# A state-space input made by channels and loaded in place, with the R transposes moved ahead of a g product

## The reference, cut to what matters

```python
z = jnp.einsum('bld,de->ble', h, w_in)
x_lru, g_lru, u_s5, gate_a, gate_b = jnp.split(z, SPLITS, axis=-1)
y_a = jax.nn.gelu(g_lru) * rg_lru(causal_depthwise_conv(x_lru, conv_w, conv_b), wa, ba, wx, bx, lam)
y_s = jax.nn.gelu(s5_ssm(u_s5, a_re, a_im, b_re, b_im, c_re, c_im, d, log_dt))
# s5_ssm: 64 groups of 16 channels, 64 complex states each
#   h[t] = abar * h[t-1] + B u[t];   y[t] = Re(C h[t]) + d * u[t]
```

## Time and profile before

| | |
|---|---|
| median of 3 runs | 1422.58 us |
| profiled execution: its time, its span | 1421.72 us, 1420.0 us |
| TensorE busy | 1365.6 us (96%) |
| VectorE busy | 976.5 us (69%) |
| ScalarE busy | 697.5 us (49%) |
| GpSimd busy | 450.6 us (32%) |
| 163.7 to 227.9 us (one turn): TensorE, VectorE, ScalarE, GpSimd busy | 62.82, 57.73, 37.07, 21.87 us of 64.20 |

### The profile page before, as it was taken

The page is one execution under the profiler, slowest core; times in us unless marked ns, Lnnn a source line. Parts: engine busy times, 40 slices in busy tenths (PEclk is TensorE's granted clock), DMA queues, the critical chain, the costliest instruction groups (busy, mean ns, idle before and its releaser), DMA issues.

```text
span 1420.0 us, 19593 instructions
## 1 busy us (share of the span) xinstructions
PE 1365.6 (96%) x6615; PEld 980.0 (69%) x6615; DVE 976.5 (69%) x1443; ACT 697.5 (49%) x994; POOL 450.6 (32%) x359
## 2 busy tenths in 40 slices
PE   8999999999999999999999999999999999999991
PEld 6777877767788888874646666666666666666660
DVE  6889898977211112559437888887888878788875
ACT  5246474658222223110025766766666766666661
POOL 0004142325344443000001332344434344554420
PEclk9999999999999999999999999999999999999996
DMA  9044355343233334640068999999999999999964
GB/s 261 19 123 82 84 100 83 82 67 96 82 92 98 105 97 173 260 193 1 9 251 319 349 372 353 366 361 374 369 370 370 367 370 370 370 364 366 373 223 133
DMA packets 140918, 315.82 MB, mean 222 GB/s; under 512 B 18128, under 2 KB 99712, under 8 KB 115456
## 3 DMA queue, kind: packets, MB, share of 16 engines
q1 hardware_dynamic: 126528, 281.50, 57.1%
q0 software_dynamic: 14336, 33.59, 9.9%
HBM read 297.27 MB, written 34.54 MB: 234 GB/s over the span
## 4 chain that ended last, share of the span: by engine, by line
PE 69%; DMA 14%; DVE 8%; ACT 3%; issue 3%; DVEq 2%; SPq 1%; POOL 1%; ACTq 0%; POOLq 0%
PE bank L724 16%; PE bank L726 16%; PE bank L725 16%; DMA gate_up<-moe_w_up_in 12%; PE bank L1118 5%; PE bank L731 4%; PE bank L905 3%; DVE arena L1460 3%; PE bank L983 2%; DVEq L1457 2%; DVE arena L1466 2%; PE bank L1003 1%; ACT gate_up_high L1183 1%; PE bank L1077 1%; ACT arena L1183 1%
## 5 line engine op out<-in xcount | busy, mean ns | idle before, releaser
L1460 DVE TENSOR_TENSOR gate_up_low<-gate_up,gate_up_high 128x1024 fp32r<-128x1024 f32 x256 | 296.5, 1221 | 93.3 <-ACT gate_up_high L1183 93.3
L1183 ACT ACTIVATE gate_up_high<-gate_up 128x1024 fp32r<-128x1024 f32 x256 | 249.7, 1049 | 89.7 <-DMA gate_up<-moe_w_up_in 89.5
L1183 ACT ACTIVATE arena<-bank 96x512 f32<-96x512 f32 (+5 forms) x244 | 128.8, 553 | 237.5 <-PE bank L726 116.2
L673 POOL DMA_INDIRECT acc_dram<-arena x64 | 116.6, 1822 | 320.7 <-DMA acc_dram<-arena 287.7
L724 PE MATMUL bank<-gate_up_high,rows_high 128*96 128x512 f32 x512 | 206.2, 403 | 5.5 <-DVE rows_low L1460 4.8
L1460 DVE TENSOR_TENSOR arena<-arena 128x512 f32<-128x512 f32 (+11 forms) x300 | 195.7, 687 | 15.9 <-ACT arena L1183 3.2
L726 PE MATMUL bank<-gate_up_high,rows_low 128*96 128x512 f32 x512 | 202.7, 396 | 0.0
L725 PE MATMUL bank<-gate_up_low,rows_high 128*96 128x512 f32 x512 | 200.9, 392 | 0.0
L731 PEld LDWEIGHTS bank<-arena 96*128 96x128 f32 (+5 forms) x1001 | 127.1, 186 | 56.6 <-issue 38.5
L599 POOL TENSOR_TENSOR wb_low<-arena,wb_high 128x1024 fp32r<-128x1024 f32 (+1 forms) x38 | 100.5, 2646 | 152.5 <-ACT wb_high L1183 152.5
L731 PE MATMUL bank<-arena 96*128 96x96 f32 (+5 forms) x1001 | 127.8, 266 | 9.7 <-DMA arena<-x_in 6.6
(11 more groups left out here) (172 smaller groups left out, 2586.1 us busy)
## 6 DMA issues: line engine op xcount, KB each, us to landing
gate_up<-moe_w_gate_in SPq DMA_DIRECT2D x64, 1024.0 KB, 18.5
gate_up<-moe_w_up_in SPq DMA_DIRECT2D x64, 1024.0 KB, 21.1
down<-moe_w_down_in SPq DMA_DIRECT2D x64, 1024.0 KB, 16.2
arena<-w_in_in SPq DMA_DIRECT2D x40, 512.0 KB, 4.1
arena<-w_glu_in SPq DMA_DIRECT2D x16, 512.0 KB, 3.9
arena<-w_lru_out_in SPq DMA_DIRECT2D x8, 768.0 KB, 4.8
arena<-x_in SPq DMA_DIRECT2D x8, 512.0 KB, 5.3
wu<-w_in_in SPq DMA_DIRECT2D x8, 512.0 KB, 7.8
```

What stands on the lines that cost most here:

```text
L673: nc.gpsimd.indirect_dma_start(out=acc_dram, out_offset=bass.IndirectOffsetOnAxis(ap=idxcol[:, 4 + c:5 + c].bitcast(u32), axis=0), in_=yb[ ...
L1183: return nc.scalar.activation(out_, in_, func, **kw)
L1460: return V_.tensor_tensor(out_, a, b_, op)
```

## The change

U is made by channels (channels on the partitions, tokens in the free dimension). The stationary operand of each matmul is now the weight tile, the moving one x. The first four channel tiles are made in two passes of 256 tokens each, with the k steps outside and the four tiles inside; the last four as before in one piece of 512 columns. Banks of the start are dealt anew. ScalarE's copy reorders the tokens: chunk c, step l goes to position l x 64 + c. `u_dram` is channels by tokens, and eight DMAs per block, one for each step l, load it straight into U; they are issued after the Y products of the block before. U2, U2g, ScalarE's reordering, the 16 U transposes and the two bank copies of a block are gone. The R transposes and the wait for them stand ahead of g product 0. The wait of g product 0 in the first block for the powers moves to x product 2. GpSimd no longer waits for the U transposes.

```diff
-        u_dram = dram("u_dram", (T, D))
+        u_dram = dram("u_dram", (D, T))
...
-        usb = at(rt_off, TT * D).rearrange("p (t d) -> p t d", t=TT)
+        usb = at(rt_off, KD * T).rearrange("p (n x) -> p n x", n=KD)
...
-        U_BANKS = [1, 2, 3, 4, 5, 0, 6, 7]
-        BC_BANKS = [6, 7, 1, 2]
+        U_BANKS = [0, 1, 2, 3, 5, 4, 6, 7]
+        BC_BANKS = [6, 7, 0, 1]
...
-            def load_u2(b):
-                sp.dma_start(U2, u_dram.rearrange("(c l) x -> c l x", l=L)[:, :, b * GB * GP:(b + 1) * GB * GP]
-                             ).then_inc(S["u2_loaded"], 16)
+            def load_u(b):
+                for l in range(L):
+                    sp.dma_start(U[l * GP:(l + 1) * GP],
+                                 u_dram[b * GB * GP:(b + 1) * GB * GP, l * NC:(l + 1) * NC]
+                                 .rearrange("(g o) c -> o g c", o=GP)).then_inc(S["U_loaded"], 16)
...
-            sp.dma_start(u_dram.rearrange("(t p) d -> p t d", p=P), usb).then_inc(S["u_stored"], 16)
+            sp.dma_start(u_dram.rearrange("(n p) x -> p n x", p=P), usb).then_inc(S["u_stored"], 16)
...
-                    sp.wait_ge(S["yT_put"], 2 * (b + 1))
-                    load_u2(b + 1)
+                    sp.wait_ge(S["Y_put"], 2 * (b + 1))
+                    load_u(b + 1)
...
                 pool.wait_ge(S["RT_put"], 4 * (b + 1))
-                pool.wait_ge(S["U_put"], 2 * (b + 1))
...
+            def u_part(k, m, th):
+                xs = slice(th * 256, (th + 1) * 256)
+                ms = slice(m * P, (m + 1) * P)
+                return mm3(banks[U_BANKS[m]][:, xs], wu_hi[k // 2][:, k % 2, ms], wu_lo[k // 2][:, k % 2, ms],
+                           xH[k][:, xs], xL[k][:, xs], th == 0 and k == 0, th == 1 and k == KD - 1)
...
-            u_proj(0)
+            pe.wait_ge(S["low_ready"], 4)
+            for k in range(KD):
+                if k % 2 == 0:
+                    pe.wait_ge(S["wu_low"], k // 2 + 1)
+                for m in range(4):
+                    u_part(k, m, 0)
             pe.wait_ge(S["rows_loaded"], 16 * 7)
-            tp(banks[0][:, 0:112], rows, 112)
-            tp(banks[0][0:GP, P:P + G], drow, G).then_inc(S["rows_put"], 1)
+            pe.wait_ge(S["low_ready"], 2 * TT)
+            tp(banks[4][:, 0:112], rows, 112)
+            tp(banks[4][0:GP, P:P + G], drow, G).then_inc(S["rows_put"], 1)
...
-            u_proj(1)
-            u_proj(2)
-            bc_turn(0)
-            u_proj(3)
+            for k in range(KD):
+                if k == 6:
+                    bc_turn(0)
+                for m in range(4):
+                    last = u_part(k, m, 1)
+                    if k == KD - 1:
+                        last.then_inc(S["u_put"], 1)
             bc_turn(1)
             u_proj(4)
...
-                if b == 0:
-                    pe.wait_ge(S["powers_kept"], 1)
-                g_proj(0)
-
-                pe.wait_ge(S["U2_turned"], b + 1)
                 need(pe, "yT_kept", 2 * b)
-                for g in range(GB):
-                    last = tp(banks[4 + g // 8][:, (g % 8) * NC:(g % 8 + 1) * NC], U2g[:, g, :], NC)
-                    if g % 8 == 7:
-                        last.then_inc(S["U_put"], 1)
-
                 pe.wait_ge(S["R_ready"], b + 1)
-                pe.wait_ge(S["U_kept"], 2 * (b + 1))
                 need(pe, "Y_kept", 4 * b)
                 for n in range(2 * QB):
                     q, c = divmod(n, 2)
                     last = tp(banks[4 + n // 4][:, (n % 4) * P:(n % 4 + 1) * P], R[:, c, q, :], P)
                     if n % 4 == 3:
                         last.then_inc(S["RT_put"], 1)
+                g_proj(0)
...
                 pe.wait_ge(S["K_ready"], b + 1)
+                pe.wait_ge(S["U_loaded"], 16 * L * (b + 1))
...
             def u_kept(n):
-                hf, t = divmod(n, TT)
                 act.wait_ge(S["u_put"], n + 1)
-                f(usb[:, t, hf * 512:(hf + 1) * 512], banks[U_BANKS[n]][:, :], ACT.Copy).then_inc(S["u_kept"], 1)
+                f(usb[:, n, :].rearrange("p (l c) -> p c l", l=L), banks[U_BANKS[n]][:, :].rearrange("p (c l) -> p c l", l=L),
+                  ACT.Copy).then_inc(S["u_kept"], 1)
...
-                        act.wait_ge(S["u2_loaded"], 16 * (b + 1))
-                        if b == 0:
-                            act.wait_ge(S["u_stored"], 16)
-                        need(act, "Y_put", 2 * b)
-                        f(U2g.rearrange("c g (l o) -> c l g o", l=L),
-                          U2.rearrange("c l (g o) -> c l g o", g=GB), ACT.Copy).then_inc(S["U2_turned"], 1)
...
-                for s in range(2):
-                    act.wait_ge(S["U_put"], 2 * b + s + 1)
-                    f(U[:, 8 * s:8 * s + 8, :].rearrange("p g c -> p (g c)"), banks[4 + s][:, :], ACT.Copy).then_inc(S["U_kept"], 1)
```

More of the change, by code:

```diff
@@ L176, in decoder_layer @@
         uy_off = top[0]
-        U2 = at(uy_off, L * GB * GP, NC).rearrange("p (l x) -> p l x", l=L)
-        Y2 = U2
+        Y2 = at(uy_off, L * GB * GP, NC).rearrange("p (l x) -> p l x", l=L)
         new(L * GB * GP)
@@ L182, in decoder_layer @@
         RT = new(2 * QB * P).rearrange("p (q c x) -> p q c x", q=QB, c=2)
-        U2g = at(top[0], GB * P, NC).rearrange("p (g x) -> p g x", g=GB)
         M = new(GB * P).rearrange("p (g x) -> p g x", g=GB)
@@ L442, in _ @@
             sp.wait_ge(S["u_stored"], 16)
-            load_u2(0)
+            load_u(0)
             for b in range(NB):
@@ L740, in _ @@
                     last.then_inc(S["xT_put"], 1)
+            def u_part(k, m, th):
[3 more added lines that the diff above has]
+                           xH[k][:, xs], xL[k][:, xs], th == 0 and k == 0, th == 1 and k == KD - 1)
             def u_proj(n):
-                hf, t = divmod(n, TT)
-                if hf == 0:
-                    pe.wait_ge(S["low_ready"], 2 * t + 2)
+                ms = slice((n - 4) * P, (n - 3) * P)
                 if n == 5:
@@ L748, in u_proj @@
                     pe.wait_ge(S["bc_kept"], 4)
-                ts_ = slice(t * P, (t + 1) * P)
                 for k in range(KD):
-                    c = 4 * hf + k // 2
-                    if t == 0 and k % 2 == 0:
+                    c = 4 + k // 2
+                    if n == 4 and k % 2 == 0:
                         pe.wait_ge(S["wu_low"], c + 1)
-                    last = mm3(banks[U_BANKS[n]][:, :], xH[k][:, ts_], xL[k][:, ts_], wu_hi[c][:, k % 2], wu_lo[c][:, k % 2],
+                    last = mm3(banks[U_BANKS[n]][:, :], wu_hi[c][:, k % 2, ms], wu_lo[c][:, k % 2, ms], xH[k], xL[k],
                                k == 0, k == KD - 1)
                 last.then_inc(S["u_put"], 1)
-            u_proj(0)
+            pe.wait_ge(S["low_ready"], 4)
[4 more added lines that the diff above has]
+                    u_part(k, m, 0)
             pe.wait_ge(S["rows_loaded"], 16 * 7)
-            tp(banks[0][:, 0:112], rows, 112)
-            tp(banks[0][0:GP, P:P + G], drow, G).then_inc(S["rows_put"], 1)
+            pe.wait_ge(S["low_ready"], 2 * TT)
+            tp(banks[4][:, 0:112], rows, 112)
+            tp(banks[4][0:GP, P:P + G], drow, G).then_inc(S["rows_put"], 1)
             def bc_turn(c):
                 if c < 2:
-                    pe.wait_ge(S["low_ready"], 2 * TT)
                     pe.wait_ge(S["b_loaded"], 16 * 2)
@@ L786, in _ @@
                     n = 2 * (j - 1) + c
-                    tp(banks[3][:, n * NQ:(n + 1) * NQ], pr[:, j, c, :], NQ)
+                    tp(banks[2][:, n * NQ:(n + 1) * NQ], pr[:, j, c, :], NQ)
             for n, v in enumerate((8, 10, 7, 3, 2)):
-                last = tp(banks[4][:, n * NQ:(n + 1) * NQ], sm[:, v, :], NQ)
+                last = tp(banks[3][:, n * NQ:(n + 1) * NQ], sm[:, v, :], NQ)
             last.then_inc(S["powers_put"], 1)
@@ L796, in x_proj @@
                     pe.wait_ge(S["v_split"], m + 1)
+                    if m == 2:
+                        pe.wait_ge(S["powers_kept"], 1)
                 elif m < 2:
@@ L1508, in _ @@
             dve.wait_ge(S["rows_put"], 1)
-            V_.tensor_copy(chan, banks[0][:, 0:112])
-            V_.tensor_copy(dT, banks[0][0:GP, P:P + G])
+            V_.tensor_copy(chan, banks[4][:, 0:112])
+            V_.tensor_copy(dT, banks[4][0:GP, P:P + G])
             d()
@@ L1597, in _ @@
             dve.wait_ge(S["powers_put"], 1)
-            V_.tensor_copy(pw[:, 1:L + 1].rearrange("p j c q -> p (j c q)"), banks[3][:, :])
-            V_.tensor_copy(misc.rearrange("p v q -> p (v q)"), banks[4][:, 0:5 * NQ])
+            V_.tensor_copy(pw[:, 1:L + 1].rearrange("p j c q -> p (j c q)"), banks[2][:, :])
+            V_.tensor_copy(misc.rearrange("p v q -> p (v q)"), banks[3][:, 0:5 * NQ])
             V_.memset(pw[:, 0, 0, :], 1.0)
```

5 lines of the change are left out of this document (2 added, 3 removed).

## The result

The changed kernel takes 1441.80 us (median of 4 runs, 1438.79 to 1443.16) against 1422.46 for the kernel before beside it (4 runs, 1418.55 to 1422.94): ratio 1.0138, 95% interval 1.0124 to 1.0152. It is slower by 19.3 us, where the forecast had +3.5 and a range that ended at 1431.

A forecast was written before the change was run, and what follows sets the result against it. TensorE bounds until about 46 us, VectorE from 47.24 to 99.50, mostly TensorE from 105, with VectorE having little to spare. 5.55 + 0.3 + 2.0 - 4.3 = +3.5 us: 1426.1 for the median, range 1420 to 1431.

The forecast's parts named there:

- Start: Up to the first S products: late VectorE low part, then a lower TensorE clock; S products 7.85 us later.
- VectorE's loss: Before the first S products: late low part 5.55, copy beside GpSimd's memset 0.3; 5.85 us.
- Third rival: First 107 us: short matmuls bound by the weight load, 173 at 0.19; +15.6, 1438 us; chance 0.07.
- Fourth rival: U load: small-run loads land late, over 30 us, and S products wait; chance 0.06 together with the unseen.
- First rival: Block 0: same mechanism, but TensorE's clock doesn't fall in the new gap; +1.5, 1424.1 us; chance 0.22.
- VectorE's turn: Blocks 1 to 3: waits of 2.5 us go, GpSimd overlap costs 1.2; net 1.3 a turn, 4.3 in all.
- The upper bound of 1.9: Blocks 1 to 3: most that GpSimd's low parts beside the tables would cost VectorE; 1.9 us.
- the 1.8 us saved "at full contention": Blocks 1 to 3: low bound of the three turns' saving, no high-part wait saved, full contention; 1.8 us.
- The clock: Block 0, g product 1: TensorE at lower clock after 5.5 us idle; 2.0 us, bounds 0 and 3.4.
- Second rival: Blocks 1 to 3: every turn gains TensorE's whole 2.5 us; -1.8, or -3.3 with cheaper copies; chance 0.20.
- The rest of the turn: Blocks 1 to 3: VectorE's waits that could go, 0.6, 0.33, 0.70 and 0.9; together 2.5 us a turn.
- the extra that the forecast gave the first turn: First of the three turns: 1.6 us saved instead of 1.3, counting a somewhat longer wait.

The follow-up runs named there:

- experiment 5: Changed kernel with 24 unread matmuls of 512 columns between g product 0 and the wait for the Q tables: 1435.38 us.
- experiment 3: Changed kernel with GpSimd's low parts of blocks 1 to 3 held until the Q tables are ready: 1424.07 us.
- experiment 4: Changed kernel with only the second of GpSimd's two low parts of a turn held until the Q tables are ready: 1433.05 us.
- experiment 1: Changed kernel with its R transposes back behind g product 0: 1420.93 us.
- experiment 7: Changed kernel, R transposes behind g product 0, high parts before U copies: 1419.56 us; also with constant rows and first B turn earlier: 1418.17 us.
- experiment 8: Second version of experiment 7 with g product 1 split around the S products and GpSimd's memset ahead of its low parts: 1418.69 us.

## Why the prediction was wrong, step by step

- **Start, right.** Short matmuls at 0.12 (0.119 measured), rows turned at 25.4 (25.05), copies from 38.3 (38.11) at 1.05 each (0.99), low part at 42.6 (41.96), S products +7.85 (+7.9). Inside the sum, VectorE's loss was 5.85 and is 5.02, the clock's was 2.0 and is 2.9 (8.53 against 5.66 us; experiment 5 agrees). The two misses cancel, and that the sum is right to 0.1 us is luck.
- **Third rival, wrong**, as argued: short matmuls are not bound by the weight load. **Fourth rival, wrong**: the U load lands in 2.5 us (its row among the DMA issues of after, 140 to 200 us: KB each, median us to landing) and the S products never wait for it. The longest landing of all the U loads is 7.4, still more than 20 us ahead of the S products that read it. **First rival, wrong**: the clock fell in the new gap. (The third rival counts 173 short matmuls where the sum above it has 96 + 87 = 183; it changes nothing here.)

```profile
arena<-u_dram SPq DMA_DIRECT2D x8, 64.0 KB, 2.5
```

- **VectorE's turn, the step that failed.** It read "2.7 us of overlap costs about 1.2 (bounds 0 and 1.9)". Measured: 4.2 (experiments 3 and 4). The error is one of kind. I took a slowdown in proportion to the overlap, from a low part of VectorE that took 2.11 beside GpSimd. The trace already held the answer: 0.9 is no rate but a stop, until GpSimd's first multiplication ended at 132.95.

```profile
131.91 1.04 POOL L628 TENSOR_TENSOR arena<-arena 128x512 f32<-128x512 f32 x1 [2.49 <-DVEq L1457]
```

  With a stop, the price is not set by how long the two streams lie beside each other but by GpSimd's operations that a table product meets, 2.0 to 2.2 us for each low part of 2.35. There are two. The 2.7 us of overlap is itself too short by the prediction's own rows: from 219.8 to the end of the closing operation, 221.88 + 1.36 = 223.24, are 3.4. The overlap was also longer than I placed it, because a stopped VectorE is still in its tables when the second low part starts: 163.26 to 169.13 lies wholly inside the tables' 157.38 to 170.35. The upper bound of 1.9 was thus no bound. Nor was the 1.8 us saved "at full contention": 3 x (2.5 - 0.7 - 1.9) is a loss of 0.3, and 1.8 comes out only with 1.2 of contention.
  The Trainium skill (SBUF — State Buffer, "SBUF: two separate sides") states it: a GpSimd operation that reads SBUF and a VectorE operation with two inputs in SBUF take a shared pair of ports as an exclusive lock for the whole instruction, and the one that comes second "fully blocks". This case's trace agrees (3.55 us for one product of 1.36, none longer than 1.36 with GpSimd held back). By it the term would have been 2 x 2.35 = 4.7, an estimate, near the 4.2 measured; the sum did not weigh it.
- **The clock, counted once instead of four times.** The sum has TensorE's idle time only in block 0. But a gap of TensorE ahead of the K products follows from my own step: with R turned early nothing is left between g product 0 and the tables. With the contention that I forecast it would have been some 2.2 us (1.0 and 1.2), and no run has a gap of that length there; with the measured contention it was 5.20. That wait put the clock to its 1.2 GHz level in each turn: 2.5 us in the second block (6.16 against 3.67 for the K products), 2.1 and 1.8 in the next.
- **Second rival's premise, wrong in a way the sum missed.** I let all of TensorE's 2.5 us count as a possible gain of the early R. But the K products also wait for the tables. In the first turn these were ready at 159.32 (157.96 + 1.36) and the K products started at 159.83; in the second, at 223.24 and 224.01. As long as the tables come when they do, nothing put ahead of that wait could start the K products more than 0.5 to 0.8 us earlier. VectorE's chain sets a floor for each turn, and experiments 1 and 3 meet it with R behind and R ahead alike, at 62.5.

```profile
157.96 1.36 DVE L1466 SCALAR_TENSOR_TENSOR arena<-arena 128x1152 f32<-128x1152 f32 x1
159.83 3.67 PE L880 MATMUL bank<-arena 64*16 64x128 f32 x64 [0.45 <-ACT arena L1183]
```

- **The rest of the turn, 0.8 us too good.** The forecast was 62.9 with 1.2 of contention. Without contention that is 61.7, and 62.5 was measured: of the 2.5 us of waits 1.7 were saved. TensorE's busy time alone is 61.47 (experiment 7), so the second rival's 61.7 was just about its floor.

The terms add up: 62.5 + 4.2 + 2.5 = 69.2 for the first turn of 69.1, 68.8 with the 2.1 of the second (68.7), 68.5 with the 1.8 of the third (68.5). Of the 18.1 us between the forecast for the three turns (-4.3) and what they took (+13.8), 9.0 are contention (3 x 3.0), 6.4 the clock, and 2.4 savings that did not come (3 x 0.8). The remaining 0.3 is the extra that the forecast gave the first turn.

## What to carry to other kernels

Before moving work ahead of a wait, name what the work behind the wait needs last: if it is another engine's result, the move gains no more than the time between that result and the present start, and it may start third engines early. Price VectorE beside GpSimd by whole operations and not by overlap: for each multiplication or subtraction of GpSimd's that meets one of VectorE's with both inputs in SBUF, count nearly its whole length as lost, and hold it back where VectorE is critical. (A plain copy of VectorE's stops too, as the next section has it.) And where a wait as long as these (5 us, and in most cases 3) is made on TensorE, add the clock's loss behind it, at every repetition.

## What the runs showed of the hardware

- VectorE's table products (two inputs in SBUF) stop for a GpSimd subtraction of 128x1024: 2.2 us of one of 2.35. GpSimd stops for them too (3.46 us instead of 2.35). The nine convolution steps, which read one input from a bank, took 7.01 us in the kernel before, with GpSimd's low parts beside them, and 7.01 in the changed one, where those parts were already done. ScalarE's high parts beside the tables cost nothing.
- One input in SBUF is no protection for a plain copy: VectorE's copy of 128x512 behind the convolutions takes 0.42 us alone, 1.34 to 1.61 beside GpSimd's memset in the kernel before, and 1.06 beside a low part in experiment 8. At 230.29 it ends 0.28 us after the memset, at 166.63 in experiment 8 0.28 us after the low part. Where the low parts run early, it is back at 0.42.
- The granted clock after a wait: 5.2 to 5.5 us of idle TensorE lowered it in block 0 and in the three turns of after, to 0.50 over a whole stretch of 5 us in block 0 and the second block, to 0.62 and 0.53 at the lowest in the next two; five or so us later it was back. A wait of 3.2 us, the same in three turns of one kernel, lowered it in two and not in one. In block 0 of other runs waits of 2.80 and 2.81 us left it at 1.00 (experiment 7) and one of 2.75 went with 0.66 (experiment 8); from 20 us on, waits of 1.64 us and less left it at 1.00 throughout. What tells these apart stays open.
- Matmuls of 256 columns, with 128x128 weights loaded for each, start 0.119 us apart, a little over half of the 0.23 of 512.
- ScalarE's copy of 128x512 from a bank takes 0.99 us when it writes every 64th element and 0.52 when it writes them in a row.
